# Three output projections joined with the following input projection, the embedding products of one stage moved ahead, and the last attention steps scaled on VectorE

## The chip, the cores and the metric

One core of a Trainium2 chip runs the whole program. The metric is the device time of one execution in microseconds; lower is better. The engines are named as in the profile: PE (TensorE matmuls), PEld (its weight loads), DVE (VectorE), ACT (ScalarE), POOL (GpSimd), SP (the queue that issues the transfers).

## The reference

Five transformer layers over one sequence of 512 tokens, model width 1024, all in fp32. The first layer is

```
h = x + 0.5 * rms(swiglu(rms(x)))                            # ffn1
h = h + rms([rms(stick_breaking(q,k,v)), rms(chunk_band(q,k,v))] @ w_out)   # mix
h = h + 0.5 * rms(swiglu(rms(h)))                            # ffn2
e = (p @ w_ple_proj) * sigmoid(h @ w_ple_gate)               # ple, p is 512 x 256
h = h + rms(e)
```

and then come four layers `x = x + mixer(rms(x) * w)`, whose mixers are a gated convolution (conv), a forgetting attention (fox), a gated delta rule (gdn) and a sliding window attention with sinks (swa). Each mixer is an input projection, something in the middle, and an output projection that is added to the residual. A final rms norm ends it.

## The kernel before

Everything is held feature by token: `h`, `F` and the split inputs `xh`, `xl` are 128 x 8 x 512, that is eight blocks of 128 features. Weights come from memory in tiles of 1024 x 128 (512 KB). Fp32 accuracy is had by splitting each operand in a rounded high half and the rest: `split_hi` on ACT writes `wh`, `split_lo` on DVE writes `wl`, and a block is three matmuls, `wh*xh`, `wh*xl`, `wl*xh` (`mm3`). A weight tile is thus 8 x 3 = 24 matmuls of 512 columns. There are 4 raw buffers and 4 split buffers; a tile is split 3 tiles ahead (HEAD = 3) of its use, and its transfer is issued 4 tiles ahead, when the low half of the buffer's last tile is written.

Each engine has its own instruction list, written stage by stage in the order of the code, and engines meet through semaphores. A stage is a `Block`; at its end all engines wait for one another before any of them goes on (lines 899, 542, 1700, 1717 in the profile are such ends).

A stage that needs a new input begins with a `Prologue`: for each of the 8 blocks ACT writes `xh` (L392) and DVE writes `xl` (L422 or L425); where the block before ended in an rms norm, DVE first scales `F` by the norm (L406) and DVE (even blocks, L410) or POOL (odd blocks, L438) adds it to `h`. The first three weight tiles are then multiplied together, block by block (`head_mm`, L457, L458, L461), so that PE can begin with the first block. The norm's mean square is had by adding squares of the blocks: squares on ACT, additions on POOL (L450, L447), and the last sum over partitions on PE (`sums_pe`, L335: one half for the added squares, one for the last square), then `inverse_dve` (L342 to L347), `root_act` (L351), and `spread_pe` (L357), which spreads the result over the partitions.

`resid_out` is the output projection of the conv, fox and gdn mixers (and swa): eight tiles; after each, DVE adds the PSUM bank to `h` (L930) and ACT squares the new block (L917). `in_proj` is the next stage: in a `Block` of its own its prologue writes `xh`, `xl` from `h`, and PE begins with the 16 small matmuls of `sums_pe`.

The ple stage has 16 weight tiles, gate and projection by turns. A projection tile has only 256 rows, so 6 matmuls and a split of a quarter of the size. At the stage's start `p` is loaded, turned by 8 PE transposes (L1776) and split (L1733, L1757); the gate tiles go through a sigmoid (L1743), are multiplied with the projection (L1766) and squared (L1747).

`pair_steps` is a pipeline for softmax attention over pairs of heads and blocks of 128 queries (the chunk band attention `ch` of the mix stage, 16 steps, and the swa attention): scores on PE (L1233), mask and maximum on DVE (L1269), exponential on ACT (L1302), reciprocal of the row sum on DVE (L1280), scaling of the probabilities on POOL (L1293), transposes on PE (L1241), a copy out of PSUM on ACT (L1316 or L1310), and the product with the values on PE (L1251). Most steps stand between the tiles of the input projection; the last ones (the tail) have no weight tiles beside them. After `ch`, POOL squares the four output groups and adds them (`out_sums`, L1615, L1620), and the output projection `mix_out` starts with the sum over partitions (`x_pe`, L1658).

## Time and profile before

| what | value |
|---|---|
| median of 3 runs | 2294.39 us (2293.29 to 2296.99) |
| the profiled execution's own time | 2293.49 us |
| its span in the trace | 2291.8 us |
| mean granted TensorE clock | 0.966 of full |
| PE busy | 2186.6 us, 95% of the span |
| DVE, ACT, POOL busy | 49%, 38%, 18% |
| DMA, mean over the span | 79 GB/s |

The page gives a start and a duration for each instruction; a matmul of 512 columns shows 0.39 us, but matmuls overlap, and their starts are closer than that. What counts for PE is the distance between starts. Times "us" in rows are from the start of the span.

### The profile page before, as it was taken

To read this page: it belongs to the slowest core of one execution; us is meant where nothing else is said; L and a number is where in the kernel's file an instruction comes from. 1 tells how busy PE (TensorE), PEld (TensorE's weight loads), DVE (VectorE), ACT (ScalarE), POOL (GpSimd) and SP (SyncE) were. 2 spreads that over 40 slices of the span, in tenths; PEclk is the share of its full clock that TensorE was granted. 3 is DMA by queue.
4 is the path that set the end of the run, shared out by engine and by line. 5 is a ranking of instruction groups with operands and counts; after the bars stand their busy time and mean duration, and the time that the engine had idled before them with its cause. 6 is when DMAs were issued, how large, how long until landed. Compare 5 with 4: busy or idle time off the path is not lost. (4 is left out here: it accounts for less than half of the span.)

```text
span 2291.8 us, 29105 instructions
## 1 busy us (share of the span) xinstructions
PE 2186.6 (95%) x10770; PEld 1766.9 (77%) x10770; DVE 1130.7 (49%) x1796; ACT 867.3 (38%) x1424; POOL 423.1 (18%) x462
## 2 busy tenths in 40 slices
PE   7999999999889999998899999999999999999989
PEld 6888887766577888887788877886778888876657
DVE  5444324544446444323475544336656686665443
ACT  4322223564334323222432232125446743433453
POOL 2111002113423111001120010002100342024441
PEclk9999999999989999999999999999999997999999
DMA  4333334511022333331233336650243221243102
GB/s 141 110 100 92 100 98 88 98 46 56 19 74 78 106 93 99 92 101 53 86 109 93 92 74 104 87 96 7 66 115 88 56 56 29 77 104 65 47 16 68
DMA packets 359321, 182.11 MB, mean 79 GB/s; under 512 B 41925, under 2 KB 356014, under 8 KB 358830
## 3 DMA queue, kind: packets, MB, share of 16 engines
q1 hardware_dynamic: 358872, 180.57, 30.9%
q8 instruction: 67, 1.10, 0.2%
q14 instruction: 40, 0.33, 0.0%
q10 hardware_dynamic: 342, 0.12, 0.0%
HBM read 176.14 MB, written 4.52 MB: 79 GB/s over the span
## 5 line engine op out<-in xcount | busy, mean ns | idle before, releaser
L313 PE MATMUL ps<-xh,wh 128*128 128x512 f32 x1920 | 764.9, 398 | 3.4 <-DVE F L1766 2.0
L315 PE MATMUL ps<-xh,wl 128*128 128x512 f32 x1920 | 749.9, 391 | 0.0
L314 PE MATMUL ps<-xl,wh 128*128 128x512 f32 x1920 | 749.1, 390 | 0.0
L280 DVE TENSOR_TENSOR wl<-raw,wh 128x1024 fp32r<-128x1024 f32 x334 | 423.0, 1267 | 437.7 <-ACT wh L270 433.5
L270 ACT ACTIVATE wh<-raw 128x1024 fp32r<-128x1024 f32 x334 | 342.3, 1027 | 364.8 <-PE ps L315 315.9
L313 PEld LDWEIGHTS ps<-xh,wh 128*128 128x128 f32 x1920 | 361.2, 188 | 86.7 <-issue 10.7
L315 PEld LDWEIGHTS ps<-xh,wl 128*128 128x128 f32 x1920 | 361.1, 188 | 77.2
L314 PEld LDWEIGHTS ps<-xl,wh 128*128 128x128 f32 x1920 | 361.3, 188 | 73.5 <-issue 2.4
L457 PE MATMUL ps<-xh,wh 128*128 128x512 f32 x304 | 132.4, 436 | 24.7 <-ACT xh L392 8.1
L450 POOL TENSOR_TENSOR acc<-acc,sq 128x512 f32<-128x512 f32 x72 | 102.5, 1423 | 275.0 <-ACT sq L866 178.0
L315 PE MATMUL ps<-a_hi,wl 128*128 128x512 f32 x352 | 137.0, 389 | 0.0
L314 PE MATMUL ps<-a_lo,wh 128*128 128x512 f32 x352 | 137.0, 389 | 0.0
L313 PE MATMUL ps<-a_hi,wh 128*128 128x512 f32 x352 | 137.0, 389 | 0.0
L777 POOL TENSOR_TENSOR F<-F,rstd 128x512 f32<-128x512 f32 x44 | 57.1, 1298 | 398.7 <-ACT F L793 398.7
L458 PE MATMUL ps<-xh,wl 128*128 128x512 f32 x304 | 129.1, 425 | 0.0
L457 PEld LDWEIGHTS ps<-xh,wh 128*128 128x128 f32 x304 | 64.3, 212 | 41.1 <-issue 19.2
L461 PE MATMUL ps<-xl,wh 128*128 128x512 f32 x304 | 92.6, 413 | 2.3 <-DVE xl L422 1.7
L796 ACT ACTIVATE a_hi<-ps 128x512 f32 (+1 forms) x44 | 26.3, 598 | 163.3 <-DVE ps L817 163.3
L447 POOL COPY acc<-sq 128x512 f32<-128x512 f32 x12 | 8.7, 728 | 406.0 <-ACT sq L917 319.6
L793 ACT ACTIVATE F<-ps 128x512 f32<-128x512 f32 x44 | 26.3, 598 | 149.6 <-DVE ps L814 149.6
L313 PEld LDWEIGHTS ps<-a_hi,wh 128*128 128x128 f32 x352 | 66.1, 188 | 13.8
L314 PEld LDWEIGHTS ps<-a_lo,wh 128*128 128x128 f32 x352 | 66.1, 188 | 13.8
(388 smaller groups left out, 2558.5 us busy)
## 6 DMA issues: line engine op xcount, KB each, us to landing
raw<-in_w_ffn_gate SPq DMA_DIRECT2D x44, 512.0 KB, 3.8
raw<-in_w_ffn_up SPq DMA_DIRECT2D x44, 512.0 KB, 3.8
raw<-in_w_ffn_down SPq DMA_DIRECT2D x32, 512.0 KB, 3.6
raw<-in_conv_w_in SPq DMA_DIRECT2D x32, 512.0 KB, 4.0
raw<-in_fox_w_in SPq DMA_DIRECT2D x32, 512.0 KB, 9.6
raw<-in_gdn_w_in SPq DMA_DIRECT2D x32, 512.0 KB, 4.1
raw<-in_w_in SPq DMA_DIRECT2D x24, 512.0 KB, 3.8
raw<-in_swa_w_in SPq DMA_DIRECT2D x32, 256.0 KB, 3.7
```

The source lines that it names most:

```text
L270: nc.scalar.activation(wh[s][:, 0:kb, :], raw[r][:, 0:kb, :], ACT.Copy).then_inc(hi_done, 1)
L280: nc.vector.tensor_tensor(wl[s][:, 0:kb, :], raw[r][:, 0:kb, :], wh[s][:, 0:kb, :].bitcast(F32), ALU.subtract).then_inc(lo_done, 1)
L313: pe.matmul(o, wh[s][:, kb, :], x_hi, start=start, stop=False)
L314: pe.matmul(o, wh[s][:, kb, :], x_lo, start=False, stop=False)
L315: return pe.matmul(o, wl[s][:, kb, :], x_hi, start=False, stop=stop)
L450: nc.gpsimd.tensor_tensor(acc[:, :], acc[:, :], sq[:, b % 2, :], ALU.add).then_inc(acc_done, 1)
L457: pe.matmul(ps[g][:, :], wh[s][:, b, :], x_hi[:, b, :], start=b == 0, stop=False)
L458: pe.matmul(ps[g][:, :], wl[s][:, b, :], x_hi[:, b, :], start=False, stop=False)
L461: last = pe.matmul(ps[g][:, :], wh[(t + g) % SPLIT][:, b, :], x_lo[:, b, :], start=False, stop=b == DB - 1)
L777: nc.gpsimd.tensor_tensor(SR[:, s, :], S[:, s, :], rstd[:, :], ALU.mult).then_inc(sr_done, 1)
L793: nc.scalar.activation(S[:, s, :], ps[ffn_bank(i, j)][:, :], ACT.Silu).then_inc(silu_done, 1)
L796: nc.scalar.activation(act_hi[:, bass.ds(p, 1), :], ps[ffn_bank(i, j)][:, :].rearrange("p (o q) -> p o q", o=1), ACT.Copy).then_inc(up_hi, 1)
```

## The change

Four parts.

1. **Joins.** `conv_out` with `fox_in`, `fox_out` with `gdn_in` and `gdn_out` with `swa_in` share one `Block` each. Inside the last tile of the output projection ACT writes `xh` of blocks 0 to 6 as soon as PE has read the old `xh` block for the last time (new semaphore `x_free`), and DVE writes `xl` of blocks 0 to 5, before it adds the last tile to `h`. Blocks 6 and 7 follow after that. PE goes straight on with the first three tiles of the next projection; the sums stand between its blocks 1 and 2. SP and POOL wait for the whole new `xl` before they issue anything of the new stage.
2. **Embedding products first.** The 8 projection tiles of ple (256 x 128 each) are packed in 2 tiles. `p` is loaded into `F[6:8]` at the end of `ffn2_up`, turned after the ninth of the 24 tiles of `ffn2_down` and split there. Two of the eight products stand at the end of `ffn2_down`, between the halves of the sums and before the spread; six at the start of ple. ACT copies them to `pp`; two gate tiles are split inside the prologue, and the gate's head starts when that is done.
3. **Tails on VectorE.** The scaling of the last 3 steps of `ch` and of the last 2 of swa goes from POOL to DVE.
4. **Last square.** The square of the last output group of `ch` is made on DVE, and it isn't added to the others: PE sums it in PSUM, with 8 more small matmuls.

The number of 512-column matmuls is the same.

```diff
+        def p_load(sp):
+            sp.wait_ge(h_new, n["h"])
+            sp.wait_ge(h_pool, n["h"])
+            sp.dma_start(pt, I["p"][0, 0].rearrange("(t p) d -> p t d", p=P)).then_inc(p_in, 16)
...
+        def p_turn(pe, k):
+            if k != P_AT:
+                return
+            pe.wait_ge(p_in, 16)
+            for b in range(2):
+                for t in range(TB):
+                    m = pe.transpose(ps[6 + b][:, t * P:t * P + P], pt[:, t, b * P:b * P + P], ident[:, :])
+                m.then_inc(p_t, 1)
+
...
+        def p_product(pe, o):
+
+            t, m = first["ple"] + o // 4, o % 4
+            pe.wait_ge(lo_done, t + 1)
+            if o == 0:
+                pe.wait_ge(p_lo, 2)
+            if o >= 3:
+                pe.wait_ge(p_hi, 2 + o - 2)
+            for q in range(2):
+                last = mm3(pe, p_bank(o)[:, :], t % SPLIT, 2 * m + q, phi[:, q, :], plo[:, q, :], q == 0, q == 1)
+            last.then_inc(*((tile_done, 1) if m == 3 else (p_t, 1)))
+
...
+                up0 = ffn_up(block, "ffn2_up", gains("g_ffn2_pre"), gains("g_mix_post"), a_hi, a_lo, p_load)
+                post_out(block, "ffn2_down", a_hi, a_lo, DOWN, x_at=lambda xb: (evac, up0 + 2 * xb + 2),
+                         amid=dict(pe=p_turn, act=p_split_hi, dve=p_split_lo),
+                         between=(lambda pe: p_product(pe, 0), lambda pe: p_product(pe, 1)))
...
+                    p_out(0)
+                    p_out(1)
+                    pro.act(act, {1: lambda e: (p_out(2), p_out(3)), 2: amid_2, 3: lambda e: p_out(5), 4: amid_4, 5: lambda e: p_out(7)})
...
+                    pro.dve(dve, {3: lambda e: split(0), 5: lambda e: split(1)})
...
+                    for o in range(2, DB):
+                        p_product(pe, o)
+                    t = t0 + PACKED
+                    pe.wait_ge(lo_done, t + HEAD)
+                    for b in range(DB):
+                        head_mm(pe, range(HEAD), t, b, pro.x0, xh, xl)
+                    for o in range(HEAD, DB):
+                        s = (t + o) % SPLIT
+                        pe.wait_ge(lo_done, t + o + 1)
+                        wait(pe, evac, ev0 + o - 3 if o > 3 else 0)
...
+        def sums_pe(pe, acc_at, sq_at, between=None):
 
             for q, src in enumerate((acc[:, :], sq[:, 1, :])):
+                if q and between is not None:
+                    between(pe)
...
+                    if joined is not None:
+                        pe.wait_ge(evac, ev0 - 1)
                     for b in range(kb):
+                        if joined is not None and b == 2:
+                            sums_pe(pe, *joined)
...
+                    elif frees and o == DB - 1:
+                        last.then_inc(x_free, 1)
...
+                    if joined:
+                        sp.wait_ge(xs_lo, pro.x0 + DB)
...
+                    if joined:
+                        root_act(act, st)
...
+                        if k == DB - 1 and pro is not None:
+                            for b in range(DB - 1):
+                                act.wait_ge(x_free, xf0 + b + 1)
+                                pro.high(act, b)
...
+                        if k == DB - 1 and pro is not None:
+                            for b in range(DB - 2):
+                                pro.low(dve, b)
...
+                    if u >= N - last:
+                        dve.wait_ge(p_scaled, B + 2 * u)
+                        dve.wait_ge(ri_done, B + 2 * u + 2)
+                        for h in range(2):
+                            z = zbuf(u, h)
+                            nc.vector.tensor_scalar(z, z, cols[:, RI, 2 * u + h:2 * u + h + 1], None, ALU.mult).then_inc(p_scaled, 1)
 
             def pool_step(pool, s):
                 if sink is not None and s < N:
@@ -1285,7 +1349,7 @@
                         pool.wait_ge(t_done, B + 2 * (s - R) + 2)
                     k = pairs[s]["klen"]
                     nc.gpsimd.tensor_copy(Z[:, s % R, :, k:k + 1].rearrange("p h o -> p (h o)"), sink[0](s)).then_inc(e_sink, 1)
-                if 1 <= s < N + 1:
+                if 1 <= s < N - last + 1:
...
+                dve.wait_ge(o_taken, g_ch + 4)
+                dve.wait_ge(n_sq, 7)
+                dve.wait_ge(n_sum, 3)
+                nc.vector.tensor_tensor(osq[:, 3, :], F[:, 7, :], F[:, 7, :], ALU.mult).then_inc(n_sq, 1)
...
-                pe.wait_ge(n_sum, 6)
+                pe.wait_ge(n_sum, 5)
                 for g in range(2):
                     for t in range(TB):
-                        m = pe.matmul(ps[6][:, g * TB + t:g * TB + t + 1], osum[:, g, t * P:t * P + P], ones[:, 0:1],
-                                      start=True, stop=True)
+                        pe.matmul(ps[6][:, g * TB + t:g * TB + t + 1], osum[:, g, t * P:t * P + P], ones[:, 0:1],
+                                  start=True, stop=g == 0)
+                        if g:
+                            pe.wait_ge(n_sq, 8)
+                            m = pe.matmul(ps[6][:, g * TB + t:g * TB + t + 1], osq[:, 3, t * P:t * P + P], ones[:, 0:1],
+                                          start=False, stop=True)
```

How the instruction lists move, first at the join of `fox_out` with `gdn_in`, on DVE. Before (L930 adds a tile to `h`, L280 splits a weight tile, L425 writes `xl`, L342 to L347 and L363 are the norm):

```order
L280 TENSOR_TENSOR wl<-raw,wh 128x1024
L930 TENSOR_TENSOR h<-ps,h 128x512
L899 UNCONDITIONAL_BRANCH
L575 UNCONDITIONAL_BRANCH
L425 SCALAR_TENSOR_TENSOR xl<-h,vA,xh 128x512 x2
L342 TENSOR_SCALAR rms_col<-ps 128x4
L344 SCALAR_TENSOR_TENSOR rms_col<-ps,rms_col 128x4
L347 RECIPROCAL rms_col<-rms_col 128x4
L425 SCALAR_TENSOR_TENSOR xl<-h,vA,xh 128x512 x4
L363 COPY rstd<-ps 128x512
L425 SCALAR_TENSOR_TENSOR xl<-h,vA,xh 128x512 x2
L280 TENSOR_TENSOR wl<-raw,wh 128x1024
```

In the change (the same instructions are L984, L287, L437, L351 to L356 and L372):

```order
L287 TENSOR_TENSOR wl<-raw,wh 128x1024
L984 TENSOR_TENSOR h<-ps,h 128x512
L287 TENSOR_TENSOR wl<-raw,wh 128x1024
L437 SCALAR_TENSOR_TENSOR xl<-h,vA,xh 128x512 x6
L984 TENSOR_TENSOR h<-ps,h 128x512
L437 SCALAR_TENSOR_TENSOR xl<-h,vA,xh 128x512 x2
L606 UNCONDITIONAL_BRANCH
L351 TENSOR_SCALAR rms_col<-ps 128x4
L353 SCALAR_TENSOR_TENSOR rms_col<-ps,rms_col 128x4
L356 RECIPROCAL rms_col<-rms_col 128x4
L372 COPY rstd<-ps 128x512
L287 TENSOR_TENSOR wl<-raw,wh 128x1024
```

Six of the eight `xl` blocks moved ahead of the last addition to `h`, the other two right behind it, and the norm and the next weight split are no longer among them.

Second, the start of ple on DVE. Before (L406 scales `F`, L410 adds to `h`, L422 writes `xl`, L1757 splits `p`, L280 splits a weight tile):

```order
L406 SCALAR_TENSOR_TENSOR F<-F,half,ps 128x512
L410 TENSOR_TENSOR h<-F,h 128x512
L406 SCALAR_TENSOR_TENSOR F<-F,half,ps 128x512
L1757 TENSOR_TENSOR p_lo<-ps,p_hi 128x512 x2
L406 SCALAR_TENSOR_TENSOR F<-F,half,ps 128x512
L410 TENSOR_TENSOR h<-F,h 128x512
L422 TENSOR_TENSOR xl<-h,xh 128x512
L406 SCALAR_TENSOR_TENSOR F<-F,half,ps 128x512
L422 TENSOR_TENSOR xl<-h,xh 128x512
L406 SCALAR_TENSOR_TENSOR F<-F,half,ps 128x512
L410 TENSOR_TENSOR h<-F,h 128x512
L422 TENSOR_TENSOR xl<-h,xh 128x512
```

In the change (L415, L419, L434, L287):

```order
L415 SCALAR_TENSOR_TENSOR F<-F,half,ps 128x512
L419 TENSOR_TENSOR h<-F,h 128x512
L415 SCALAR_TENSOR_TENSOR F<-F,half,ps 128x512 x2
L419 TENSOR_TENSOR h<-F,h 128x512
L434 TENSOR_TENSOR xl<-h,xh 128x512
L287 TENSOR_TENSOR wl<-raw,wh 128x1024
L415 SCALAR_TENSOR_TENSOR F<-F,half,ps 128x512
L434 TENSOR_TENSOR xl<-h,xh 128x512
L415 SCALAR_TENSOR_TENSOR F<-F,half,ps 128x512
L419 TENSOR_TENSOR h<-F,h 128x512
L434 TENSOR_TENSOR xl<-h,xh 128x512
L287 TENSOR_TENSOR wl<-raw,wh 128x1024
```

The split of `p` is gone from here, and two splits of whole gate tiles stand inside the prologue; the second one, for which the gate's head waits on PE, is behind five scalings, three additions and three `xl` blocks.

Third, the tail of `ch` on DVE. Before (L1269 is the mask and maximum, L1273 and L1280 make the negated maximum and the reciprocals, L1260 copies the output group):

```order
L1269 ISA ch_room,ch_cols<-ps,bias 128x512
L1269 ISA ch_cols 128x1
L1273 TENSOR_SCALAR ch_cols<-ch_cols 128x2
L1280 RECIPROCAL ch_cols<-ch_cols 128x2 x2
L1260 COPY F<-ps 128x512
L542 UNCONDITIONAL_BRANCH
```

In the change (the same are L1327, L1331, L1338, L1318):

```order
L1331 TENSOR_SCALAR ch_cols<-ch_cols 128x2
L1338 RECIPROCAL ch_cols<-ch_cols 128x2
L1344 TENSOR_SCALAR ch_room<-ch_room,ch_cols 128x384 x2
L1338 RECIPROCAL ch_cols<-ch_cols 128x2
L1344 TENSOR_SCALAR ch_room<-ch_room,ch_cols 128x512 x2
L1318 COPY F<-ps 128x512
L1646 TENSOR_TENSOR out_squares<-F 128x512
L562 UNCONDITIONAL_BRANCH
```

The two scalings of each of the last steps (L1344) and the last square (L1646) stand on DVE.

## Rows read from the trace of the kernel before

**Rows 1.** The page: its head, and the split of weights on DVE (busy, mean ns).

```profile
span 2291.8 us, 29105 instructions
...
L280 DVE TENSOR_TENSOR wl<-raw,wh 128x1024 fp32r<-128x1024 f32 x334 | 423.0, 1267 | 437.7 <-ACT wh L270 433.5
```

**Rows 2.** The timeline of PE at the end of conv_in (start, duration).

```profile
1325.65 0.39 PE L314 MATMUL ps<-xl,wh 128*128 128x512 f32 x1
...
1326.56 0.39 PE L315 MATMUL ps<-xh,wl 128*128 128x512 f32 x1
1330.14 0.47 PE L457 MATMUL ps<-xh,wh 128*128 128x512 f32 x1 [3.19 <-ACT xh L945]
```

**Rows 3.** Windows: length, PE, PEld, DVE, ACT, POOL busy (count), granted clock, DMA.

```profile
714.00:724.00 10.00, 10.00 (x55) 8.57 (x55) 5.77 (x8) 3.68 (x5) 3.28 (x2) 1.00 0.18 52
1330.00:1334.00 4.00, 3.86 (x10) 3.08 (x11) 3.98 (x7) 4.00 (x8) 0.00 (x0) 0.57 0.86 253
1672.71:1688.21 15.50, 13.80 (x58) 11.60 (x57) 5.35 (x10) 8.08 (x12) 1.45 (x5) 0.78 0.67 208
```

**Rows 4.** The timeline of PE from fox_out to gdn_in.

```profile
1672.48 0.39 PE L315 MATMUL ps<-xh,wl 128*128 128x512 f32 x1
...
1688.19 0.48 PE L457 MATMUL ps<-xh,wh 128*128 128x512 f32 x1
```

**Rows 5.** Timelines of PE, ACT and DVE from conv_out to fox_in.

```profile
1375.12 0.39 PE L315 MATMUL ps<-xh,wl 128*128 128x512 f32 x1
...
1390.99 0.48 PE L457 MATMUL ps<-xh,wh 128*128 128x512 f32 x1
...
1380.79 3.77 ACT L392 ACTIVATE xh<-h,vA 128x512 fp32r<-128x512 f32 x6
...
1374.38 1.40 DVE L280 TENSOR_TENSOR wl<-raw,wh 128x1024 fp32r<-128x1024 f32 x1 [1.72 <-ACT wh L270]
...
1381.53 2.74 DVE L425 SCALAR_TENSOR_TENSOR xl<-h,vA,xh 128x512 fp32r<-128x512 f32 x4 [0.88 <-ACT xh L392]
```

**Rows 6.** The timeline of PE in ple, start and end.

```profile
1065.53 0.95 PE L335 MATMUL ps<-ones,acc 128*128 128x1 f32 x8
...
1068.38 1.12 PE L357 MATMUL ps<-ident,rms_col 128*128 128x128 f32 x4 [0.95 <-ACT rms_col L351]
1073.79 1.97 PE L1776 MATMUL ps<-ident,p_tokens 128*128 128x128 f32 x8 [4.29 <-DMA p_tokens<-in_p]
...
1137.21 0.95 PE L335 MATMUL ps<-ones,acc 128*128 128x1 f32 x8
1140.29 1.87 PE L335 MATMUL ps<-ones,sq 128*128 128x1 f32 x8 [2.13 <-ACT sq L1747]
```

**Rows 7.** The timeline of DVE in ple's prologue.

```profile
1069.82 0.75 DVE L406 SCALAR_TENSOR_TENSOR F<-F,half,ps 128x512 f32<-128x512 f32 x1 [1.79 <-PEq L1700]
...
1077.03 0.73 DVE L406 SCALAR_TENSOR_TENSOR F<-F,half,ps 128x512 f32<-128x512 f32 x1
...
1083.84 0.74 DVE L406 SCALAR_TENSOR_TENSOR F<-F,half,ps 128x512 f32<-128x512 f32 x1
```

**Rows 8.** Groups of instructions by form: scaling on POOL and on DVE.

```profile
L1293 POOL TENSOR_SCALAR ch_room<-ch_room,ch_cols 128x512 f32<-128x512 f32 x8 | 12.4, 1564 | 11.3 <-DVE ch_cols L1280 11.3
...
L1156 DVE TENSOR_SCALAR fox_qkvz<-fox_qkvz,fox_cols 128x512 f32<-128x512 f32 x8 | 3.9, 487 | 0.3
```

**Rows 9.** Timelines of POOL and PE in the tail of ch.

```profile
624.90 5.54 POOL L1293 TENSOR_SCALAR ch_room<-ch_room,ch_cols 128x384 f32<-128x384 f32 x4 [2.62 <-DVE ch_cols L1280]
...
638.69 1.26 POOL L1620 TENSOR_TENSOR out_square_sums<-out_square_sums,out_squares 128x512 f32<-128x512 f32 x1
...
640.45 3.55 PE L1658 MATMUL ps<-ones,out_square_sums 128*128 128x1 f32 x16 [3.72 <-PEq L542]
```

**Rows 10.** The timeline of POOL in the tail of swa.

```profile
2222.41 3.62 POOL L1293 TENSOR_SCALAR swa_z<-swa_z,swa_cols 128x256 f32<-128x256 f32 x4 [2.50 <-DVE swa_cols L1280]
```

**Rows 11.** DMA issues from 1340 to 1440 us (last: us to landing).

```profile
raw<-in_fox_w_in SPq DMA_DIRECT2D x17, 512.0 KB, 12.1
```

More of the change, by code:

```diff
@@ L40 @@
 DOWN = -(-FB // WB)
+PACKED = 2
 PLE = 256
@@ L297, in steps @@
             full = n // 4
-            if full < 4 or name in ("swa_in", "mix_in", "gdn_in") or name.endswith("_down"):
+            if full < 4 or name in ("swa_in", "mix_in", "gdn_in", "ple") or name.endswith("_down"):
                 for k in range(n):
@@ L541, in in_proj @@
             tails, beside = dict(tails), dict(beside)
-            with nc.Block() as block:
+            with ExitStack() as own:
+                if not joined:
+                    block = own.enter_context(nc.Block())
                 @block.sync
                 def _(sp):
+                    if joined:
+                        sp.wait_ge(xs_lo, pro.x0 + DB)
                     if "sp" in tails:
@@ L898, in resid_out @@
             x_ready = n["x"] - DB
-            with nc.Block() as block:
+            pro, xf0 = None, n["xf"]
+            if gain is not None:
+                pro = Prologue(gain, None, squares=False)
+                n["xf"] += DB - 1
+            with ExitStack() as own:
+                block = (own if joint is None else joint).enter_context(nc.Block())
                 @block.sync
@@ L931, in _ @@
                     steps(dve, name, body)
+                    if pro is not None:
+                        for b in (DB - 2, DB - 1):
+                            pro.low(dve, b)
                 @block.tensor
                 def _(pe):
-                    pe_tiles(pe, name, xh, xl, ev0, x_ready=x_ready, x_pe=x_pe)
-            return acc0 + DB - 1, sq0 + DB
+                    pe_tiles(pe, name, xh, xl, ev0, x_ready=x_ready, x_pe=x_pe, frees=pro is not None)
+            sums = (acc0 + DB - 1, sq0 + DB)
+            return sums if pro is None else (sums, block, pro)
         def split_x(src):
@@ L1739, in body @@
[L1739 to L1748 removed]
+                        act.wait_ge(tile_done, t0 + PACKED + o + 1)
@@ L2043, in _ @@
                         act_p(act)
-            sums = resid_out("fox_out", *gate_x(lambda b: qkv[:, 24 + b, :]))
+            joint = ExitStack()
+            sums, block, pro = resid_out("fox_out", *gate_x(lambda b: qkv[:, 24 + b, :]),
+                                         gain=vA[:, col["norm_w_2"] + 2 * DB:col["norm_w_2"] + 3 * DB], joint=joint)
         with ExitStack() as c:
@@ L2733, in x_pe @@
                     ins.then_inc(o_t, 1)
-            sums = resid_out("gdn_out", x_act, x_dve, x_pe, h_ready=(h_kept, 48))
+            joint = ExitStack()
+            sums, block, pro = resid_out("gdn_out", x_act, x_dve, x_pe, h_ready=(h_kept, 48),
+                                         gain=vA[:, col["norm_w_2"] + 3 * DB:col["norm_w_2"] + 4 * DB], joint=joint)
         with ExitStack() as c:
```

203 lines of the change are left out of this document (114 added, 89 removed).

## The prediction

> **What bounds the kernel now.** I read the head of the page first: the span is 2291.8 us [rows 1], the execution itself took 2293.49 us, and PE is busy 95% of it. Next I read the timeline of PE, for what a matmul costs. Five starts in a row lie 0.91 us apart [rows 2], so a matmul of 512 columns takes 0.227 us, a weight tile of 24 of them 5.45 us, and one block of the head (9 matmuls) 2.04 us. With so full a PE nothing is to be had from the other engines but the places where PE stands still. Those I looked for along its timeline. The change touches seven of them: the three ends of `resid_out`, the entry and the exit of ple, and the tails of `ch` and swa.
>
> Then the windows, for a second cost. After a wait of 3.19 us [rows 2] the granted clock of the next 4 us is 0.57 [rows 3], so some 3.4 us of it are at 1.2 instead of 2.4 GHz. Over a join as it is now the clock is 0.78 of 15.5 us [rows 3], which costs 0.22 x 15.5 = 3.4 us on top of the wait. In the middle of a projection, where the same 16 small matmuls of the sums stand between large ones, the clock is 1.00 [rows 3]. A standstill is thus paid twice, and small matmuls alone are not.
>
> **The joins.** From the end of the last tile (its last matmul starts at 1672.48, so 1672.7) to the start of the head's fifth block at 1688.19 pass 15.5 us [rows 4]. The PE work in that is four blocks, 8.2 us; the sums, 8 in 0.95 us [rows 6], so 1.8 for both halves; and the spread, about 0.4. That is 10.4 us. The join can give 15.5 - 10.4 = 5.1 us if PE waits for nothing any more.
>
> Does it wait? At `fox_out` the weights of the next three tiles are split long before the last tile ends. ACT writes its seven `xh` blocks 0.63 us apart at most (six in 3.77 us [rows 5]) while PE frees one in 0.68 us. DVE's six `xl` blocks, 0.68 us each (four in 2.74 us [rows 5]), follow one `xh` block behind, so DVE gets to the last addition some 2.6 us after the last tile. With the addition and the square (0.7 and 0.65) the last square is there 4.1 us after it. PE wants it after two blocks and half of the sums, 4.1 + 0.9 = 5.0 us. No wait: **5.1 us**, and the same for `gdn_out`. At `conv_out` the last weight split is late: it ends at 1374.38 + 1.40 = 1375.8, when the tile ended at 1375.35 [rows 5]. PE starts 0.5 us late, the `xl` blocks run from 1375.8 to 1379.8, the square is ready at 1381.3, and PE is there at 1380.9: 0.4 us more. The window is 15.64 us [rows 5], so 15.6 - 10.4 - 0.9 = **4.3 us**. Together 14.5 us. The bounds of each are 1.5 us (the clock falls all the same, 3.4 less) and 5.5.
>
> SP now waits for all of `xl`, about 5.5 us after the last tile instead of 2.2. Behind that wait stand the loads of the fifth to seventh tile of the next stage, and in gdn a copy of `h` ahead of them. A load of fox took 12.1 us to land [rows 11], which makes 17.6 us after the tile. The fifth tile has to be there at about 10.4 + 8.2 + 5.45 - 2.6 = 21.4 us, where 2.6 are its two splits: hidden with 4 us to spare. If it weren't, one late tile would cost 1 to 2 us. POOL's constants wait as long, but nothing asks for them before the head has ended. Root and spread come well before block 5. I cost all of these at 0.
>
> **Ple.** Before, the last product of `ffn2_down` ends at 1065.53 and the sums at the other end start at 1137.21 [rows 6]: 71.7 us, for 240 large matmuls (54.5 us), one set of sums, one spread and 8 transposes. After the change:
> - Sums and two products of 6 matmuls (1.36 each) end at 1065.5 + 1.8 + 2.7 = 1070.0. Root and inverse are hidden by the second. The spread ends at 1070.4, and DVE starts the next stage 1.44 us after the spread began [rows 6, 7], so at 1071.5.
> - Six products, 8.2 us: to 1079.6. ACT has to copy each bank in time, 0.6 us each, which fits.
> - The gate's head waits for DVE's second weight split. Two blocks of the prologue take 3.4 us (6.81 for four [rows 7]). Before that split stand blocks 0 to 3, block 4 (2.0 us, without the last `xl` block of four) and two weight splits of 1.27 [rows 1]: 71.5 + 6.8 + 2.0 + 2.5 = 82.8, and 0.5 for ACT, which copies banks between. So 1083.3, and PE stands still for **3.7 us**. That is the length of the wait of rows 2, after which the clock was low for 3.4 us: 1.7 us more.
> - 192 gate matmuls, 43.6 us. With the 0.85 us that the transposes now take inside `ffn2_down` (half of 1.7, since at 1073.79 [rows 6] they ran at the low clock): 1083.3 + 43.6 + 1.7 + 0.85 = 1129.4 against 1137.2, a gain of 7.8.
> - At the exit PE used to wait 2.13 us for the last square [rows 6], between the halves of the sums. Now the square of block 6 stands behind the last sigmoid on ACT, so PE waits some 2.8 us before the first half. I take 0.6 off: **7.2 us**. Bounds: 1 (twice the standstill, and at the low clock) and 12 (none).
>
> **Tails.** A POOL scaling of 512 columns takes 1.56 us and a DVE one 0.49 [rows 8]. In `ch` POOL scales the last two steps from 624.90 to 630.44 [rows 9]. On DVE they end at about 627.5, since the last exponential isn't ready before 626.3. The rest of the chain (transposes, copy, values) then ends 3.3 us earlier. The last group's square and addition, 2.3 us on POOL ending at 639.95, become one DVE instruction of 0.7, so 1.7 more: 5.0. The 8 added small matmuls cost 0.9 to 1.8 (16 took 3.55 us at 640.45 [rows 9]): **3.7 us** net, bounds 0 and 7. In swa four scalings take 3.62 us [rows 10]; on DVE the last ends 1.3 us earlier, and the chain to the stage's end is shortened by that: **1.3 us**, bounds 0 and 2.5.
>
> One page of the notes speaks against this part: the Trainium skill (GPSIMD Engine Reference, "When to use GPSIMD") calls a one-input operation on GpSimd roughly line-rate, so that moving it would bring nothing. Rows 8 show a factor of 3.2 for the same shape, so the trace disagrees.
>
> **Sum.** 14.5 + 7.2 + 3.7 + 1.3 = 26.7 us off 2293.5, so 2266.8; the median of the runs shown lies 0.9 above the profiled execution, so **2267.7 us**. About 0.2% (4.6 us) is what can be told from no change.
>
> **Rivals.**
> - *The sums cost the clock even when joined.* For: conv_out's join keeps two short waits around 16 small matmuls. Against: the clock of 1.00 in the middle of a projection [rows 3]. Each join loses 3.4: 2278. Chance 0.14.
> - *The gate's head waits longer.* POOL's additions and ACT's copies hold the prologue back, PE stands still 6 us and more and the clock stays low twice as long: ple gives 2 instead of 7.2, 2273. Chance 0.17.
> - *Scaling on DVE is no faster than on POOL.* The tails then give nothing of the 5.0: 2272.7. Rows 8 are against it. Chance 0.03. This is the page's rule above.
> - *The joins don't overlap as written.* If `xh` waits on something else than `x_free`, and the splits take place after the tile, a join saves only the stage's end, some 1.5 us: 2278.5. Chance 0.04.
> - *Slower:* with the pauses gone, the granted clock falls to half in the dense stretches themselves, as it never does in rows 3. It decides from the point where 54 us more are at the low clock, which take back the 27 gained; at 80 us more the time is 2267.7 + 40 = 2308. Nothing in the trace has it. Chance 0.03.
>
> The forecast has the remaining 0.59. Its own bounds give 2260 to 2275; both first rivals together give 2283. The range **2259 to 2281** leaves out those ends. Faster 0.95 (each case but the last, and what lies in the tails of the others), same 0.02, slower 0.03.
>
> **What would show it.** Right: at the three joins no PE wait longer than 1 us and a clock near 1.00; the sums between the head's second and third block; the fifth block 10.4 to 11.3 us after the last tile. In ple one standstill of 3 to 4 us, ended by DVE's weight split, and sums 8 us earlier. `mix_out`'s sums 5 us earlier. Wrong: a low clock after the joined sums, PE waits for `wl` in the first tiles of fox_in, gdn_in or swa_in (late loads), or a standstill before the gate's head of over 6 us.

## The result and the profile after

The change takes 2268.06 us (median of 4 runs, 2265.86 to 2270.19); the kernel before, on the same chip, 2294.80 us. The ratio is 0.9887 (0.9876 to 0.9899), so 26.7 us are gone. A second set of runs gave 2268.39 us (2266.86 to 2271.14) and 0.9894 (0.9877 to 0.9910). Intervals of this kind are some 3 us wide to each side; smaller differences are read from the traces here.

The page of the change: its head, and the split of weights on DVE, which answers to [rows 1].

```profile
span 2268.4 us, 29009 instructions
L287 DVE TENSOR_TENSOR wl<-raw,wh 128x1024 fp32r<-128x1024 f32 x328 | 418.0, 1275 | 419.3 <-ACT wh L277 415.0
```

This profiled execution took 2270.19 us, the slowest of its four. Where the time went shows best between fixed points. In both kernels PE spreads each norm over the partitions (L357 before, L366 now), and from one start of that to the next each stage has its length, in us; the last column ends where the second half of the last sums starts. Some of the experiments below stand beside the two kernels:

| kernel | mix | ffn2 and ple | conv_in and its join | fox and its join | gdn and its join | swa, to the last sums |
|---|---|---|---|---|---|---|
| before | 283.7 | 420.1 | 220.7 | 297.2 | 354.5 | 238.0 |
| the change | 283.5 | 412.6 | 219.5 | 293.3 | 348.7 | 234.4 |
| the change again | 283.5 | 412.5 | 217.4 | 292.9 | 350.9 | 234.4 |
| u_joins | 283.5 | 412.6 | 219.1 | 297.0 | 354.0 | 235.6 |
| u_ple | 285.4 | 420.6 | 215.9 | 293.6 | 348.8 | 234.6 |
| u_scale | 285.6 | 413.4 | 214.8 | 292.8 | 350.9 | 238.0 |

**The join of fox_out with gdn_in**, PE's timeline, which answers to [rows 4]:

```profile
1663.76 0.39 PE L322 MATMUL ps<-xh,wl 128*128 128x512 f32 x1
1663.99 0.39 PE L469 MATMUL ps<-xh,wh 128*128 128x512 f32 x1
...
1668.07 0.95 PE L344 MATMUL ps<-ones,acc 128*128 128x1 f32 x8
1668.88 1.03 PE L344 MATMUL ps<-ones,sq 128*128 128x1 f32 x8
...
1674.00 0.60 PE L366 MATMUL ps<-ident,rms_col 128*128 128x128 f32 x4
1674.35 0.48 PE L469 MATMUL ps<-xh,wh 128*128 128x512 f32 x1
```

The head (L469) follows the last tile's last matmul 0.23 us later, so without any pause. The sums stand behind its second block, and the fifth block starts 10.4 us after the tile's end, where it was 15.5 [rows 4]: the 5.1 us as worked out.

**The join of conv_out with fox_in**, timelines of PE, ACT and DVE, which answer to [rows 5]:

```profile
1366.45 0.39 PE L322 MATMUL ps<-xh,wl 128*128 128x512 f32 x1
1368.97 0.50 PE L469 MATMUL ps<-xh,wh 128*128 128x512 f32 x1 [2.13 <-DVE wl L287]
...
1362.84 1.06 ACT L277 ACTIVATE wh<-raw 128x1024 fp32r<-128x1024 f32 x1 [2.33 <-DMA raw<-in_fox_w_in]
...
1367.54 1.38 DVE L287 TENSOR_TENSOR wl<-raw,wh 128x1024 fp32r<-128x1024 f32 x1 [1.72 <-ACT wh L277]
```

Here PE does wait, 2.13 us, for the head's third weight tile. Back along the chain, DVE split it last, ACT before that (at 1366.40), behind the square of the seventh tile of conv_out; and that whole chain had been held up by ACT's wait, at 1362.84, for the transfer of the second tile. The windows over the two joins, and over the first 10 us of ple's head (columns as in [rows 3]):

```profile
1082.50:1092.50 10.00, 9.96 (x37) 8.10 (x38) 8.37 (x10) 4.19 (x6) 3.33 (x2) 0.83 0.20 55
1663.99:1674.35 10.36, 10.36 (x57) 8.84 (x56) 5.05 (x10) 5.04 (x8) 1.45 (x5) 1.00 0.44 179
1368.97:1381.06 12.09, 12.09 (x56) 10.08 (x57) 6.43 (x12) 6.44 (x10) 3.58 (x4) 0.86 0.27 25
```

Without a pause the clock (third column from the end) is 1.00, though the small matmuls of the sums stand in it; after the 2.13 us it is 0.86 of 12.1, 1.7 us more. This join gave 1.2 us in this execution.

**Ple**, PE's timeline at its start and end, which answers to [rows 6]:

```profile
1078.74 0.39 PE L322 MATMUL ps<-p_hi,wl 128*128 128x512 f32 x1
1082.54 0.50 PE L469 MATMUL ps<-xh,wh 128*128 128x512 f32 x1 [3.41 <-DVE wl L287]
...
1130.51 1.18 PE L344 MATMUL ps<-ones,acc 128*128 128x1 f32 x8 [2.55 <-POOL acc L462]
1131.54 1.85 PE L344 MATMUL ps<-ones,sq 128*128 128x1 f32 x8
```

The products end at 1079.0, the head waits for DVE's second weight split until 1082.5, and at the exit the pause stands ahead of the first half of the sums. Ffn2 and ple together are 7.5 us shorter.

**The tail of ch**, PE, ACT and DVE, which answers to [rows 9]:

```profile
626.23 1.51 PE L1299 MATMUL ps<-ident,ch_room 128*128 128x128 f32 x6 [3.49 <-ACT ch_room L1380]
...
629.88 1.94 PE L1299 MATMUL ps<-ident,ch_room 128*128 128x128 f32 x8 [1.09 <-ACT ch_room L1380]
...
637.46 2.26 PE L1726 MATMUL ps<-ones,out_square_sums 128*128 128x1 f32 x10 [1.96 <-PEq L562]
...
642.14 0.56 PE L1730 MATMUL ps<-ones,out_squares 128*128 128x1 f32 x2
...
624.75 0.71 ACT L1366 ACTIVATE ch_room<-ch_room,ch_cols 128x512 f32<-128x512 f32 x1
...
625.45 0.63 ACT L1380 ACTIVATE ch_room<-ps 128x256 f32<-128x256 f32 x2
...
624.20 0.75 DVE L1344 TENSOR_SCALAR ch_room<-ch_room,ch_cols 128x384 f32<-128x384 f32 x2
...
636.30 0.69 DVE L1646 TENSOR_TENSOR out_squares<-F 128x512 f32<-128x512 f32 x1
```

DVE has scaled step 14's pair by 624.95, but its transposes start at 626.23, and what releases them is ACT's copy out of PSUM (L1380) of the step before. That copy stands behind both exponentials of the last step (L1366) on ACT. The faster scaling is ready and nobody takes it. The sums start 3.0 us earlier than in [rows 9], of which 1.1 were there before the tail began; but they are 24 small matmuls at the low clock instead of 16, take 5.2 us instead of 3.55, and end at 642.7 instead of 644.0. Of the 1.9 us the longer sums take back 1.7, and from norm to norm the mix stage gave 0.2 us.

### The profile page after: what moved, and what is told of

It is laid out like the page before. It is cut to its first block and busy times, and to the rows that moved or that the text cites. A ratio compares the mean times of both kernels' runs of the same rounds, so it can differ in the third digit from the quotient of the medians.

```text
span 2268.4 us, 29009 instructions
## 1 busy us (share of the span) xinstructions
PE 2171.8 (96%) x10778; PEld 1754.5 (77%) x10778; DVE 1132.8 (50%) x1801; ACT 869.3 (38%) x1426; POOL 409.5 (18%) x450
## 5 line engine op out<-in xcount | busy, mean ns | idle before, releaser
L287 DVE TENSOR_TENSOR wl<-raw,wh 128x1024 fp32r<-128x1024 f32 x328 | 418.0, 1275 | 419.3 <-ACT wh L277 415.0
L469 PE MATMUL ps<-xh,wh 128*128 128x512 f32 x312 | 132.2, 424 | 30.1 <-DVE wl L287 11.3
L469 PEld LDWEIGHTS ps<-xh,wh 128*128 128x128 f32 x312 | 63.7, 204 | 47.2 <-issue 19.1
L322 PEld LDWEIGHTS ps<-a_hi,wl 128*128 128x128 f32 x352 | 66.1, 188 | 13.7
```

What stands on the lines that cost most here:

```text
L287: nc.vector.tensor_tensor(wl[s][:, 0:kb, :], raw[r][:, 0:kb, :], wh[s][:, 0:kb, :].bitcast(F32), ALU.subtract).then_inc(lo_done, 1)
L322: return pe.matmul(o, wl[s][:, kb, :], x_hi, start=False, stop=stop)
L469: pe.matmul(ps[g][:, :], wh[s][:, b, :], x_hi[:, b, :], start=b == 0, stop=False)
```

## The experiments

The kernels are the change with one edit each; the names are those of the table.

### Without the joins: u_joins

The three `resid_out` calls lose `gain=` and `joint=`, and `in_proj` does its prologue and sums as before.

```diff
-            sums, block, pro = resid_out("fox_out", *gate_x(lambda b: qkv[:, 24 + b, :]),
-                                         gain=vA[:, col["norm_w_2"] + 2 * DB:col["norm_w_2"] + 3 * DB], joint=joint)
+            sums, block, pro = resid_out("fox_out", *gate_x(lambda b: qkv[:, 24 + b, :])), None, None
```

> The change without its joins: each output projection and each next input projection is a stage of its own again. Theory (from the two traces: the stretches conv_out to fox_in, fox_out to gdn_in and gdn_out to swa_in came out 1.2, 5.1 and 5.7 us shorter, less 3.5 for a clock dip elsewhere): 11 to 15 us slower than the change, ratio to before 0.9935 to 0.995, some 2279 to 2283 us; at each of the three places PE waits 3 to 4 us again and the clock is low after it. The first place differs by little (1 to 2 us), since the late loads of fox's tiles held the joined version back. Rival (the joins bring nothing, the time came from elsewhere): within 2 us of the change's 2268.

Measured: 2281.24 us (2279.80 to 2283.08), ratio 0.9949 (0.9936 to 0.9963), 13.2 us above the change. The gain of the joins is real. At fox_out the old wait is back, and from the tile's end (1663.74) to the spread pass 13.5 us instead of 10.0. PE's timeline there:

```profile
1665.59 1.02 PE L344 MATMUL ps<-ones,acc 128*128 128x1 f32 x8 [1.70 <-PEq L945]
```

The wait is 1.7 to 1.8 us at each of the three places, not the 3 to 4 that were expected. The other half of the price is the clock: 0.87 of the 13.5 us here, which is 1.8 us.

In the conv_in column, though, it is no slower than the change's own trace (219.1 to 219.5).

### The ple stage as before: u_ple

`ffn2_down`, the ple stage and its tiles are those of the kernel before; the joins and both tails are the change's.

> The change with the ple stage, its tiles and ffn2_down as they were before. Theory: 7.5 us slower than the change (the sums at ple's end come 7.5 us later), about 2275.5 us, ratio to before 0.992. Rival (the gain in ple is an accident of the clock in one trace): 0 to 3 us slower.

Measured: 2276.15 us (2274.48 to 2277.89), ratio 0.9924 (0.9910 to 0.9938), 8.1 us above the change; 8.0 in the column of ffn2 and ple. The theory holds.

### Scaling on POOL again: u_scale

```diff
-                          ... c, ((2, 3), (4, 5), OUT), last=3)
+                          ... c, ((2, 3), (4, 5), OUT), last=0)
-                          ... (lambda u: heads(0, u), lambda u: heads(1, u)), last=2)
+                          ... (lambda u: heads(0, u), lambda u: heads(1, u)), last=0)
```

> The change with the scaling of ch's and swa's last steps on POOL again; the last square stays on DVE and in PSUM. Theory: in ch the scaling on DVE brought almost nothing (0.2 to 0.5 us), since the transposes of step 14 wait for ACT's copy of step 13 out of PSUM, which stands behind both exponentials of step 15; in swa 1.3 to 3. So 1.5 to 3.5 us slower than the change, ratio to before 0.989 to 0.990; the copy of ch's last group to F comes at most 0.5 us later. Rival (my forecast's chain: POOL's scaling was what the tail waited for): ch alone loses 3.3, both 4.6 us or more.

Measured: 2273.86 us (2271.78 to 2276.00), ratio 0.9914 (0.9900 to 0.9927), 5.8 us above the change. That is more than the theory had, and by itself it would fit the rival (4.6 us or more). What decides is the trace, which gives ch and swa apart. PE's timelines in ch's tail, then in swa's, of u_scale:

```profile
625.88 1.54 PE L1299 MATMUL ps<-ident,ch_room 128*128 128x128 f32 x6 [3.97 <-POOL ch_room L1357]
...
629.57 1.94 PE L1299 MATMUL ps<-ident,ch_room 128*128 128x128 f32 x8 [1.09 <-ACT ch_room L1380]
...
2202.52 1.12 PE L1299 MATMUL ps<-ident,swa_z 128*128 128x128 f32 x4 [2.31 <-POOL swa_z L1357]
```

Counted from the spread at the start of mix_in (410.87 here, 411.24 in the change), step 14's transposes start at 215.01 and 214.99, step 15's at 218.70 and 218.64: in ch the scaling on DVE brought 0.1 us at most. The mix column is 2.1 us longer here, but so it is, at 285.4, in u_ple and in e_filler, which scale on DVE: in those three traces the clock stays low through the whole tail and mix_out's head (27.3 us), in the change's it is up for 3.5 us between (6.8 and 13.7). What ch's scaling does to that chance is not settled by these traces.

In swa PE waits for POOL for 2.31 us; in the change for DVE, 1.12 us:

```profile
2202.14 0.66 PE L1299 MATMUL ps<-ident,swa_z 128*128 128x128 f32 x4 [1.12 <-DVE swa_z L1344]
```

And the windows of the same 16 us, of the change and of u_scale:

```profile
2202.00:2218.00 16.00, 12.00 (x64) 9.22 (x65) 10.56 (x19) 10.92 (x16) 0.00 (x0) 0.89 0.34 99
```

```profile
2202.00:2218.00 16.00, 11.86 (x53) 8.92 (x54) 7.99 (x13) 9.75 (x14) 2.26 (x3) 0.68 0.28 82
```

The standstill is 1.2 us shorter, and the clock is 0.89 instead of 0.68. Together that is 3.6 us in the last column, in which both traces with POOL show 238.0 and all twelve with DVE 234.4 to 235.6. That before's trace shows 238.0 too is in part an accident: its tail is low for 6.8 us where u_scale's is for 10.2, and another 3.4 us of low clock lie ahead of the tail (from 2204.3), as they do in u_joins (235.6) and in no joined trace. Without joins DVE's scaling thus makes 2.4 us (238.0 to 235.6), with them 2.9 to 3.6 (238.0 to the 234.4 to 235.1 of the joined traces).

### Fox's first tiles from another matrix: e_aligned and e_shifted

```diff
             def src(i, j):
+                if isinstance(i, int) and i == 0:
+                    return [(0, P, rows(conv_in), j * P)]
```

> The change, but the first four tiles of fox_in (the ones that are loaded during conv_out) are read from conv's input projection, whose rows are 16384 bytes apart, instead of fox's, whose rows are 16416 bytes apart. Leaves out: these four tiles' own weights, so fox's output is of other numbers. Theory (the loads are slow because of where the rows of this matrix lie): the four loads land 4 to 6 us after their issue instead of 13 to 16, PE no longer waits 2.1 us at the join and the clock stays up: the fox stage starts 3 us earlier (1.2 becomes 4 to 5 us of gain), 2265 us. Rival (four loads in flight are slow wherever they read, or the order of splits on ACT and DVE holds the join back): they land after 12 us and more as now, no change in time, 2268.

Measured: 2267.19 us (2266.08 to 2269.24). Of the change first, then of this kernel: the DMA issues of 1340 to 1360 us with their time to landing, and the window of the first of these loads.

```profile
raw<-in_fox_w_in SPq DMA_DIRECT2D x4, 512.0 KB, 14.8
```

```profile
1343.00:1355.00 12.00, 12.00 (x55) 9.93 (x54) 6.46 (x7) 5.10 (x7) 3.87 (x3) 1.00 0.70 44
```

```profile
raw<-in_conv_w_in SPq DMA_DIRECT2D x4, 512.0 KB, 4.0
```

```profile
1343.00:1355.00 12.00, 12.00 (x55) 9.94 (x54) 6.55 (x7) 5.01 (x7) 3.88 (x3) 1.00 0.47 133
```

With the same issue times (1342.9 and 1343.0 for the first) four loads of the same size land after 4.0 us instead of 14.8. Over fox's matrix the DMA engines are busy 0.70 of the time and move 44 GB/s; over conv's 0.47 and 133 GB/s. The head follows the last tile at once, with no pause to the spread: 10.0 us, as in the join to gdn_in. The conv_in column is 215.5 instead of 219.5, 4.0 us. The cause of the join's wait is thus shown; in the medians the gain is 0.9 us, within their spread.

> As the aligned experiment (the first four tiles of fox_in read from conv's input projection, rows 16384 bytes apart), but from 8 columns, that is 32 bytes, further on. Leaves out: these four tiles' own weights. Theory (what slows a load is that the pieces of 512 bytes don't begin at a multiple of 64 bytes): the four loads take 12 us and more again. Rival (it is the distance of the rows, 16416 bytes, that spreads badly over the memory): 4 us as in the aligned experiment.

Measured (one run, 2268.72 us): the four loads land after 4.1 us (the median, as the other was 4.0), and the column is 215.5 again. The theory fell: that pieces of 512 bytes begin 32 bytes off does not slow them here. The Trainium skill (DMA: Bandwidth & Descriptors, "How a descriptor splits into AXI transactions") says that a descriptor that doesn't start at a multiple of 256 bytes fetches bytes that it doesn't use; 4.1 against 4.0 neither shows nor excludes that. By the page's table a piece of 512 bytes that begins 32 bytes off would need 17 beats of 32 bytes instead of 16 (an estimate from the page), some 6% more; nothing of the kind makes 14.8 of 4.0. What stays is fox's matrix itself: the distance of its rows, 16416 bytes (conv's: 16384, gdn's: 16448, whose loads land after 4.1 us), or where it lies in memory. Which of the two wasn't tried.

### The change once more: after_again

> The change itself once more, for a second trace and a time beside the others. From norm to norm over conv_in and the join to fox_in, the joined kernels so far took 214.6 to 219.5 us in their traces, in two heaps by how long the second load of fox took (14.2 or 16.2 us), the others 219.1 and 220.7. Theory (the landing of fox's loads varies between executions, and the join pays for it): this trace may lie in either heap, and only in the one with the late load PE waits over 1 us at the join. Rival (the difference belongs to the kernels, not to the execution): 219.5 again, wait of 2.1 us. Time 2266 to 2269 either way.

Measured: 2268.39 us; the column 217.4, between the heaps, with a wait of 1.39 us for the third tile, whose load landed after 15.4 us. The second load took 14.2 us, so by the theory PE should have waited less than 1 us: it is not the second load alone that counts. But the same kernel gave 219.5 and 217.4, so the rival fell.

The value of this join differs between executions by how fox's loads land: over the eight traces with the joined order and fox's own loads the column is 214.6 to 219.5, 216.8 in the mean, against 219.1 and 220.7 unjoined. PE's wait at the join is 0 to 2.16 us in those eight.

Some of the spread comes from ahead of the join. At the start of conv_out PE waits 3.2 us for `xh` [rows 2] in all fourteen traces, and the clock behind that is low for 3.4 us in ten of them, for 6.8 in two (e_sums_early, best) and not at all in two (u_scale, e_ptcopy, the two shortest columns of the eight). In the mean that is nearly alike with and without the join. So the join is worth 3.1 us in the mean, and the change's own trace shows the worst of it.

One of the eight, that of e_sums_early, has the longest wait and no low clock behind it:

```profile
1368.84 0.50 PE L469 MATMUL ps<-xh,wh 128*128 128x512 f32 x1 [2.16 <-DVE wl L287]
```

```profile
1368.84:1380.93 12.09, 12.05 (x62) 10.20 (x63) 7.46 (x14) 6.43 (x10) 3.58 (x4) 1.00 0.27 26
```

The change's window of the same length, behind a wait of 2.13 us, shows 0.86. Whether a wait of 2 to 3 us is paid twice is thus in part chance.

### The gate's second split earlier: e_split_early

```diff
-                    pro.dve(dve, {3: lambda e: split(0), 5: lambda e: split(1)})
+                    pro.dve(dve, {3: lambda e: split(0), 4: lambda e: split(1)})
...
-... 2: amid_2, 3: lambda e: p_out(5), 4: amid_4, 5: lambda e: p_out(7)})
+... 2: amid_2, 3: lambda e: split(1), 4: amid_4, 5: lambda e: p_out(7)})
```

(`amid_4` is now `p_out(5)` and `p_out(6)`.)

> The change with the second gate tile's split one block earlier in ple's prologue: on ACT ahead of the fourth xh block (before it stood behind it, and that block waits for POOL's addition), on DVE ahead of the fifth scaling. Theory (the gate's head waits for that split and nothing else): the split ends at 1079.7 instead of 1082.5, PE's standstill before the head is 0.5 to 1.2 us instead of 3.8, the granted clock stays up after it (1.7 us more), ple's sums come 4 to 4.6 us earlier, 2263.8 us. Rival (the head runs into blocks that aren't ready, since DVE and POOL have the same work as before): PE waits inside the head instead, the sums come less than 1.5 us earlier.

Measured: 2265.07 us (2263.36 to 2266.20), ratio 0.9865 (0.9849 to 0.9882). PE, DVE and POOL:

```profile
1080.17 0.50 PE L469 MATMUL ps<-xh,wh 128*128 128x512 f32 x1 [1.54 <-DVE wl L287]
...
1077.80 2.31 DVE L287 TENSOR_TENSOR wl<-raw,wh 128x1024 fp32r<-128x1024 f32 x1
...
1077.36 1.66 POOL L450 TENSOR_TENSOR h<-F,h 128x512 f32<-128x512 f32 x1 [3.68 <-DVE F L415]
```

Counted from the spread, the head starts 1.85 us earlier, not 2.8, since this split now takes 2.31 us where it usually takes 1.27. POOL was adding to `h` at that time, as it was when DVE's additions took 1.2 instead of 0.7. The split ends 1.1 us after POOL's addition does (at 1079.0), nearly its usual length, as if it had stood still until then. That the two hold each other up is likely from this; no run here takes POOL's addition away. The low stretch at 1083.5 is gone, and the column of ffn2 and ple is 3.6 us shorter (409.0): 1.85 + 1.7. The theory holds, PE waits nowhere inside the head; the standstill before it is 1.54 us, a little more than the 0.5 to 1.2 expected.

### PE works through the standstill: e_filler

```diff
+                    pe.wait_ge(lo_done, t0 + PACKED + 1)
+                    for r in range(2):
+                        for q in range(2):
+                            mm3(pe, ps[3][:, :], (t0 + PACKED) % SPLIT, q, phi[:, q, :], plo[:, q, :], q == 0, q == 1)
```

> The change with 12 more matmuls of 512 columns (a product into a bank that is free and is written anew later) in the 3.8 us in which PE waits for the gate's second split. Theory (a standstill of PE costs twice, by the wait and by 3.4 us at 1.2 GHz after it; PE that works through it keeps 2.4 GHz): the head still begins 3.8 us after the last product, but the low clock at 1083.5 is gone, and the sums come 1.7 us earlier although PE does 2.7 us more work. Rival (the clock falls for another reason, such as the small matmuls and the pauses before it): the low stretch stays and the sums come when they did.

Measured (one run, 2269.14 us): the head starts 12.8 us after the spread in both kernels, and a window around its start is

```profile
1082.00:1092.00 10.00, 9.30 (x41) 7.41 (x40) 9.25 (x11) 5.32 (x9) 3.34 (x2) 1.00 0.20 55
```

The clock is 1.00 where it was 0.83, and the column is 411.2 instead of 412.6: 1.3 us less time for 12 more matmuls. All nine other traces with this standstill have the low stretch behind it, and none of their columns is under 412.3. This shows directly, though in one trace, that the second price of a standstill is its low clock. (The total doesn't tell it: the mix stage of this run has the long low stretch.)

### Fewer small matmuls behind the stage's end: e_sums_early

```diff
+                    if x == f"c{CU + 1}":
...
+                        pe.wait_ge(n_sum, 5)
+                        for g in range(2):
+                            for t in range(TB):
+                                pe.matmul(ps[TURN][:, g * TB + t:g * TB + t + 1], osum[:, g, t * P:t * P + P], ones[:, 0:1],
...
-                pe.wait_ge(n_sum, 5)
-                for g in range(2):
+                pe.wait_ge(n_sq, 8)
```

> The change with 20 of the 24 small matmuls of mix_out's sums taken out of the way: the 8 for what is added up long before (both groups, without the last square) stand inside ch's tail, where PE waits, and only 4 for the last square are left behind the stage's end; DVE adds the two parts in one more small instruction. Theory (the 24 matmuls run at the low clock, 0.21 us each, from 637.5 to 642.4, with everything in mix_out behind them): 4.1 us less there, 0.3 back on DVE, mix_out's head starts 3.8 us earlier (at 641.2), 2264.3 us. Rival (something else holds mix_out's head, the table that ACT loads until 638.6 or F's scaling): 0 to 1.5 us.

(The profile counts each of these fp32 matmuls twice, which the expectation mixed up: of the 24 in the change's rows 16 move into the tail and 8 stay, not 4.) Measured: 2270.19 us (2268.73 to 2270.95), ratio 0.9888 (0.9871 to 0.9905): nothing to be seen in the total. PE's timeline:

```profile
638.31 1.84 PE L1732 MATMUL ps<-ones,out_squares 128*128 128x1 f32 x8 [1.96 <-PEq L562]
...
644.46 0.80 PE L469 MATMUL ps<-xh,wh 128*128 128x512 f32 x1 [1.41 <-ACT xh L1768]
```

The sums now take 1.84 us behind the stage's end instead of 5.2, and counted from the spread the head starts 2.7 us earlier. But the mix column is only 1.5 us shorter, at the upper end of the rival: the low clock lasts until some 650 in both traces, so the earlier head has more of it.

### ACT's copy before the exponentials: e_ptcopy

```diff
+                if last == 3 and s in (N - 2, N - 1):
+                    turned_copy(act, s)
+                    exponential(act, s)
+                    return
```

> The change with ACT's copy out of PSUM ahead of the exponentials in ch's steps 14 and 15. Theory (in the tail the transposes of step 14 wait for the copy of step 13, which stands behind the exponentials of step 15, and this ate the gain of the faster scaling): the transposes of step 14 start 1.0 to 1.3 us earlier (at 625.0 instead of 626.2), the last copy to F and the sums 1 us earlier. Rival (the exponentials are then late by as much, since the chain mask, exponential, scaling is as long): no change at the sums.

Measured (one run, 2265.00 us), PE's timeline:

```profile
624.59 1.28 PE L1299 MATMUL ps<-ident,ch_room 128*128 128x128 f32 x6 [2.27 <-DVE ch_room L1344]
...
635.70 1.63 PE L1736 MATMUL ps<-ones,out_square_sums 128*128 128x1 f32 x7 [1.96 <-PEq L562]
```

Now the scaling is what releases the transposes. Counted from the spread they start 1.2 us earlier than in the change, the sums 1.3, and the mix column is 1.1 shorter (282.5). The theory holds.

### The head without its third tile: e_join_order, and everything together: best

```diff
+                        pe.wait_ge(lo_done, t + HEAD - 1)
+                        pe.wait_ge(evac, ev0 - 1)
+                        for b in range(2):
+                            head_mm(pe, range(HEAD - 1), t, b, x_ready, x_hi, x_lo)
```

> The change, and at each join the head doesn't wait for its third weight tile: ACT and DVE make the first two blocks of xh and xl ahead of the third tile's split, PE multiplies blocks 0 and 1 for two tiles first (2.7 us of work), then for the third. Theory (the join to fox_in loses 2 to 5 us in executions with a late load, since PE stands still for up to 2.5 us and the clock falls for 3.4): no wait over 0.5 us there in any execution, conv_in to fox_in takes 214 to 215.5 us, 1 to 4 us less in the median; the two other joins stay as they are within 0.5 us. Rival (DVE's xl blocks now run late, since the split stands among them, and the last square with them): the sums behind block 1 wait, and the two other joins get 1 to 2 us longer.

Measured: 2270.10 us (2266.47 to 2273.48), ratio 0.9895 (0.9878 to 0.9912), no gain. In its trace the second load of fox took 19.2 us, and the edit has nothing against that: on ACT the `xh` blocks stand behind the split of that second tile and the square that follows it, and PE's head waits for them.

```profile
1370.00 0.58 PE L469 MATMUL ps<-xh,wh 128*128 128x512 f32 x1 [3.37 <-ACT xh L429]
```

The column is 221.0. The theory fell; the two other joins stayed as they were (292.8, 350.7), so the rival fell there too.

> The change with everything together: ACT's copy ahead of the exponentials in ch's tail, 20 small matmuls of the sums inside the tail, the gate's second split one block earlier, ple's squares ahead of the sigmoids, and the join's order. Theory: the gains are in different stages and add up: 1.1 (copy) + 1.5 (small matmuls, as measured, since half of their gain went to the low clock) + 3.6 (split) + 0.9 (square: the last one but one is ready before PE asks) + 1 to 4 (join): 8 to 11 us, 2257 to 2260. Rival (the parts hide one another, or the clock takes it back): 2263 and more.

Measured: 2263.84 us (2260.19 to 2266.61), ratio 0.9868 (0.9851 to 0.9884), the lowest median of all, 4.6 us under the change in the same set, though the intervals of the two touch. The theory (2257 to 2260) fell all the same, and the rival's 2263 and more came. The ple part gave 5.7 us (406.8). The mix part gave 1.2 (282.3) instead of 2.6: in this trace the clock is low through the whole tail, 23.9 us. The conv_in column is 2.8 us longer than the change's (222.3), in two parts. Some 1.7 are the longer low stretch ahead of the join (1312 to 1319). At the join itself the sums behind the second block wait 1.46 us for the last square, which is late because the third tile's split stands among DVE's `xl` blocks, as the rival of e_join_order had it; and the clock behind that wait is low for 6.8 us. A version without that edit wasn't run.

## Why the prediction came out

2267.7 was forecast and 2268.1 measured. That the two agree to 0.4 us is luck: two terms of the sum were wrong in opposite directions, and the traces of the two kernels are only 23.4 us apart, since the one of the change is of its slowest execution.

- **Joins, 14.5.** Taken away they cost 13.2. The working for fox_out holds to the tenth: no wait, sums between the second and third block, 10.4 us. In the columns of fox and gdn the joined traces are 293.2 and 350.2 in the mean, 3.9 and 4.1 less than the two unjoined. The 5.1 was read from a trace with much low clock at the join: 0.78 of 15.5 us, where u_joins has 0.87 of 13.5. On the other hand before has no low clock in fox_out, where u_joins and the change both have 3.4 us of it (from 1619.3 and 1619.4). For conv_out 4.3 was forecast, 3.1 is the mean, 1.2 the change's own trace.
- **The step that failed there** is "at `conv_out` the last weight split is late": 0.5 us of lateness was taken from one trace of before, and the 12.1 us of [rows 11] were used only for the fifth tile, where they do no harm. In the change the split ends 2.2 us after the tile, in e_aligned, without the slow loads, PE doesn't wait at all. The tiles that the head itself needs have the same slow loads, and their landing moves by 2 us and more between executions.
- **Ple, 7.2.** Measured 7.5 in the traces, 8.1 by u_ple. The standstill came out at 3.4 and ended with the split that was named, the half clock after it cost 1.3 (e_filler) to 1.7, and at the exit PE waited 2.55 us ahead of the first half (2.8 was said).
- **Ch's tail, 3.7: wrong, 0.2.** The step that failed is "The rest of the chain (transposes, copy, values) then ends 3.3 us earlier". It takes POOL's scaling for what the transposes wait for. (By its own ends, 630.44 and 627.5, it would have been 2.9.) They wait just as long for ACT's copy of the step before, and with u_scale the times of step 14 and 15 are the same to 0.1 us. The 1.7 us from the last square came (it ends at 637.0 instead of 639.95, less the 1.1 of earlier stages), and the 8 more small matmuls took them back: 5.2 us at the low clock instead of 3.55.
- **Swa's tail, 1.3: wrong, 3.6.** The standstill shrank by 1.2, as said; the term that was mis-sized is the clock, put at nothing: in the change it is 0.89 of 16 us, in u_scale 0.68. Of the 3.6, though, some 1.4 arise ahead of the tail and fit the low stretch at 2204.3 that only the unjoined traces have; that leaves 2.2 to the scaling in this pair, and 2.4 between before and u_joins. The prediction had this second price for the joins and for ple, and left it out here.
- The costs set at 0 (SP's and POOL's longer wait, root and spread) are 0: PE waits for no `wl` in the tiles that follow the heads of fox_in, gdn_in and swa_in.
- Of the rivals, "the sums cost the clock even when joined" fell with the window of 1.00; "scaling on DVE is no faster" fell with DVE's 0.75 us for two scalings of 384 columns, though in ch the outcome was that rival's, for another reason. The rival of joins that don't overlap is given as 2278.5; its own terms (4.5 saved instead of 14.5) make 2277.7, and nothing hangs on it.
- Of the signs, two did not come: at conv_out PE waits 2.13 us for a `wl`, where at most 1 was to be seen, and mix_out's sums are 3.0 us earlier instead of 5. Ple's sums start 6.7 us earlier where 8 was said, with the pause now ahead of them. Those of the other two joins and of ple's standstill came.

## What to carry to other kernels

A standstill of PE is mostly paid twice, by the wait and by the half clock after it (the same wait of 3.2 us was so in twelve of fourteen traces); cost every wait that a change adds or removes with both, and where one can't be removed, more work for PE in it may cost less than nothing. Before an engine's work is moved to a faster one, read what releases the next instruction if that work were free: here a copy on ACT, queued behind two exponentials, was ready no earlier. When two stages are joined, the stage's end no longer hides the loads of the first tiles; look at their time to landing, and at its spread over executions, tile by tile.

## What the runs showed of the hardware

- Loads of 512 KB from one matrix take 5.4 to 20.3 us in the change's trace, 11 in the median, where the same shape from conv's and gdn's takes 4.0 and 4.1. It comes with that matrix, not with an offset of 32 bytes.
- The same instructions keep or lose the clock by chance: in two traces of the change gdn has 348.7 and 350.9 us, and mix, with the same instructions, has 283.5 in the change and 285.4 in u_ple. Behind one and the same wait of 3.2 us of PE the clock was low for 3.4 us in ten traces, 6.8 in two and not at all in two.
- DVE's split of a weight tile took 2.31 instead of 1.27 us in a place where POOL was adding, and DVE's addition 1.2 instead of 0.7.
